# A hybrid decoder layer: second tile's projections by half rows, first experts from 64 sums, three last gathers split

## The reference

```python
def token_mix(x, positions, w_in, conv_w, conv_b, dt_bias, a_log, d_skip, norm_w, w_out):
    proj = x @ w_in
    q, k, v, iq, ik, iw, z, xbc, dt = jnp.split(proj, SPLIT_POINTS, axis=-1)
    attn = dsa_attention(q, k, v, iq, ik, iw, positions)
    ssd = ssd_mixer(z, xbc, dt, conv_w, conv_b, dt_bias, a_log, d_skip, norm_w)
    return jnp.concatenate([attn, ssd], axis=-1) @ w_out

def peer(h, wq, k1, k2, u, v):
    ...
    s1 = jnp.einsum('nhd,kd->nhk', q[:, :, 0], k1)
    s2 = jnp.einsum('nhd,kd->nhk', q[:, :, 1], k2)
    v1, i1 = lax.top_k(s1, 16)
    v2, i2 = lax.top_k(s2, 16)
    cand = (v1[..., :, None] + v2[..., None, :]).reshape(ntok, PEER_HEADS, -1)
    ...
    best, pos = lax.top_k(cand, 16)
    ...
    act = gelu(jnp.einsum('td,tkd->tk', xb, u[ib])) * gb
    return jnp.einsum('tk,tkd->td', act, v[ib])

x = layer_norm(ALPHA * x + token_mix(...))
x = layer_norm(ALPHA * x + peer(x, ...))
```

## Time and profile before

| | us |
|---|---|
| three runs | 791.58, 791.97, 792.56 |
| median | 791.97 |
| the profiled execution, whole | 791.58 |
| its span in the trace | 789.8 |

### The profile page before, as it was taken

One profiled execution on the slowest core, in us unless ns is written; L12 is line 12 of the kernel. 1 busy time (PEld: TensorE's weight loads), 2 busy tenths in 40 slices (PEclk: granted clock), 3 DMA queues, 4 the chain that ended last, 5 costly groups with the idle time before them and its releaser, 6 DMA issues.

```text
span 789.8 us, 10145 instructions
## 1 busy us (share of the span) xinstructions
PE 558.5 (71%) x3336; PEld 463.3 (59%) x3336; DVE 544.4 (69%) x1392; ACT 456.9 (58%) x818; POOL 280.6 (36%) x270
## 2 busy tenths in 40 slices
PE   8999999998977696758464546545454655465695
PEld 5486597767977596647353545545454645454642
DVE  1789479899745848484858586867667676767545
ACT  0244237878746676657565657656565656565633
POOL 0000004446633253434444444444434344434310
PEclk9999999999999899767877777677777677867699
DMA  8993019999999999999999999999999999999993
GB/s 318 387 394 159 27 55 336 397 418 421 421 418 420 421 420 420 422 422 420 422 419 424 418 422 421 421 421 421 422 420 423 420 424 420 423 420 423 421 420 126
DMA packets 49826, 301.09 MB, mean 381 GB/s; under 512 B 5221, under 2 KB 5877, under 8 KB 16249
## 3 DMA queue, kind: packets, MB, share of 16 engines
q0 software_dynamic: 37152, 268.45, 82.2%
q1 hardware_dynamic: 11448, 28.25, 9.5%
q10 hardware_dynamic: 1184, 3.88, 1.3%
HBM read 299.50 MB, written 1.06 MB: 381 GB/s over the span
## 4 chain that ended last, share of the span: by engine, by line
DMA 51%; DVE 18%; PE 16%; issue 7%; ACT 5%; POOL 2%; DVEq 0%; ACTq 0%; POOLq 0%
DMA arena<-in_expert_uv,expert 50%; PE bank L538 6%; DVE arena L1640 4%; PE bank L705 4%; PE bank L668 2%; POOL arena L498 2%; ACT arena L1089 1%; PE bank L649 1%; DVE big L1353 1%; PE bank L734 1%; ACT weight L1079 1%; ACT arena L999 1%; DMA arena<-in_w_idx 1%; PE bank L530 1%; DVE score L1623 1%
## 5 line engine op out<-in xcount | busy, mean ns | idle before, releaser
L705 PE MATMUL bank<-ident,arena 128*128 128x128 f32 x1920 | 306.0, 331 | 217.4 <-ACT arena L1089 217.4
L498 POOL DMA_INDIRECT arena<-in_expert_uv,expert x254 | 274.9, 1082 | 472.4 <-PE bank L705 244.7
L705 PEld LDWEIGHTS bank<-ident,arena 128*128 128x128 f32 x1920 | 284.2, 175 | 242.1 <-ACT arena L1089 239.8
L1640 DVE SCALAR_TENSOR_TENSOR arena<-x_sb,arena 128x1024 f32<-128x1024 f32 x256 | 307.3, 1224 | 171.2 <-DMA arena<-in_expert_uv,expert 170.9
L1089 ACT ACTIVATE arena<-arena,weight 128x1024 f32<-128x1024 f32 x240 | 257.0, 1138 | 2.2
L1074 ACT ACTIVATE gelu<-dots 128x4 f32<-128x4 f32 (+2 forms) x80 | 16.3, 204 | 222.8 <-DVE arena L1640 222.1
L1079 ACT ACTIVATE weight<-gelu,gate 128x1 f32<-128x1 f32 x256 | 56.4, 285 | 3.6
L538 PE MATMUL bank<-arena,x_t 128*128 128x512 f32 (+1 forms) x128 | 52.6, 563 | 1.3 <-DMA arena<-in_w_idx 1.3
L538 PEld LDWEIGHTS bank<-arena,x_t 128*128 128x128 f32 x128 | 24.3, 196 | 23.5 <-issue 20.1
L734 PE MATMUL bank<-arena,mid 128*128 128x512 f32 x64 | 28.6, 597 | 1.4 <-ACT mid L1086 1.4
L550 PE MATMUL bank<-x_t,arena 128*128 128x128 f32 x256 | 29.3, 276 | 0.0
(11 more groups left out here) (244 smaller groups left out, 518.7 us busy)
## 6 DMA issues: line engine op xcount, KB each, us to landing
arena<-in_w_in SPq DMA_DIRECT2D x5, 2048.0 KB, 20.4
arena<-in_w_out SPq DMA_DIRECT2D x2, 2048.0 KB, 19.9
arena<-in_expert_uv,expert POOLq DMA_INDIRECT x254, 26.7
wq_homes<-in_peer_wq SPq DMA_DIRECT2D x2, 1024.0 KB, 15.5
mix<-in_peer_wq SPq DMA_DIRECT2D x2, 1024.0 KB, 9.9
big<-in_peer_wq SPq DMA_DIRECT2D x2, 1024.0 KB, 8.9
x_sb<-in_w_q ACTq DMA_DIRECT2D x1, 1024.0 KB, 10.1
ln_gb<-in_w_q ACTq DMA_DIRECT2D x1, 1024.0 KB, 12.6
```

Of the source, the lines that this page charges most:

```text
L498: pool.indirect_dma_start(out=arena[:, slot * SLOT:(slot + 1) * SLOT], out_offset=None, in_=expert_uv, in_offset=bass.IndirectOffsetOnAxis ...
L705: last = mm(banks[2 * tile + k // 4][:, (k % 4) * P:(k % 4 + 1) * P], lhsT=arena[:, at + k * P:at + (k + 1) * P], rhs=ident[:, :], is_tran ...
L1640: ins = stt(rows, x_rows[:, bass.ds(tile * D_MODEL, D_MODEL)], 1.0, rows, ALU.mult, ALU.mult, accum_out=dots[:, parity, j:j + 1])
```

## The change

- `project_xbc` for tile 1 becomes `project_xbc_rows`: contraction step outside, column block inside, so that after half the steps the even slot is free. A semaphore `half_weights_read` counts this for xbc0, xbc1, z and v; slots 10, 12, 14 and 4 wait for it and no longer for the whole job.
- Three steps of xbc0 stand where one column block stood, a fourth where `carry_state` stood. `T_b` and `carry_state`, with their copies on ACT, come later. The second half of v, `carry_state` and the transposes of the probabilities change places with sums of slots.
- `first_slots`: slot 4 is the seventh, slot 1 the tenth.
- `name_first_pairs`: the first eight experts are named from the 8 x 8 sums of the best 8 of each side, before the next 8 are searched. (The best 8 of all 256 sums are among these 64.)
- Both convolutions of tile 1 stand behind the first dots.
- The last three gathers are split into u and v halves, not two.

```diff
-    start = [10, 11, 12, 13, 14, 15, 1, 10, 11, 12, 13, 5, 4, 14, 15, 0]
...
+    start = [10, 11, 12, 13, 14, 15, 4, 10, 11, 1, 12, 13, 5, 14, 15, 0]
...
+        HALVES_READ = {10: 1, 12: 2, 14: 3, 4: 4}
...
+                        elif slot in HALVES_READ:
+
+                            pool.wait_ge(half_weights_read, HALVES_READ[slot])
...
-            gather_unit(UNITS - 1, 1, SLOTS - 2)
+            gather_unit(UNITS - 1, 1, SLOTS - LAST_APART)
...
+                    if job in (("proj_z", 1), ("proj_v", 1)) and k == KT // 2 - 1:
+                        last.then_inc(half_weights_read, 1)
...
+            def project_xbc_rows(t, n, ks=range(KT)):
+
+                job = ("proj_xbc", t, n)
+                if ks[0] == 0:
+                    wait_bank(pe, job)
+                for k in ks:
+                    for c in range(4):
+                        last = mm(bank(job)[:, c * P:(c + 1) * P], lhsT=weight_rows(f"xbc{n}", k)[:, c * P:(c + 1) * P],
+                                  rhs=x_t[:, k, t * P:(t + 1) * P], start=k == 0 and c == 0, stop=k == KT - 1, skip_group_check=True)
+                    if k == KT // 2 - 1:
+                        last.then_inc(half_weights_read, 1)
...
-                    carry_state()
+                    project_xbc_rows(1, 0, range(3, 4))
...
-            transposes(("T_b",), [xbc[:, 4 + g, 0:P] for g in range(GROUPS)])
+            project_xbc_rows(1, 0, range(0, 3))
             logits_of(1, range(0, 2))
-            project_xbc(1, 0, range(0, 1))
...
-            project_xbc(1, 0, range(1, 4))
-            project_xbc(1, 1)
+            project_xbc_rows(1, 0, range(4, KT))
+            project_xbc_rows(1, 1)
             project(("proj_z", 1), "z", 1)
             running_sums(1)
+            transposes(("T_b",), [xbc[:, 4 + g, 0:P] for g in range(GROUPS)])
+            project(("proj_v", 1), "v", 1, ks=range(0, 4))
...
+            def name_first_pairs():
+
+                few = view(mid, 2048, 8, 8)
+                link(tt(few, top_v[:, 0, 0:8].unsqueeze(2).broadcast_to([P, 8, 8]),
+                        top_v[:, 1, 0:8].unsqueeze(1).broadcast_to([P, 8, 8]), ALU.add))
...
+                name_experts(0, range(0, 8), 8).then_inc(first_experts, 1)
```

## The result

| | us, median | lowest to highest | runs |
|---|---|---|---|
| kernel before | 791.58 | 790.02 to 792.56 | 7 |
| changed kernel | 794.89 | 793.31 to 795.26 | 7 |

The ratio of the times is 1.0041 (95% interval 1.0030 to 1.0051): **3.3 us slower**, outside the forecast range and on the side that was given 14%. The profiled execution took 794.75 us, with a span of 793.0 us, against 789.8.

The account below looks back on a forecast made before the run. The DMA stream of 256 gathers of 1 MB at about 420 GB/s was taken as the bound. Span 789.8 - 0.3 (25th gather) + 0.2 (tail) = 789.7 us, median forecast 791.9 us, eight in ten 789.8 to 793.9.

Parts of the forecast that it names:

- the side that was given 14%: Whole kernel: the chance 0.14 that the change makes it slower by more than 0.2%, 1.6 us here.
- First gather: Chain up to the first gather's issue: 0.4 + 2.1 + 1.0 = 3.5 us earlier, at 114.1 us.
- Slots by halves: Gathers behind the first, released by half projections: third at 116.7 us, seventh at 130.7 us instead of 133.3.
- The stand-still: PE ahead of tile 1's attention: waits 2.72 us for ACT's copies from 146.15 us; attention then takes 3.6 us.
- Where the lead goes: 19th to 25th gathers, behind tile 1's attention: of 3.5 us of lead, 0.3 us is left at the 25th landing.
- the engines ran dry: DMA at the 21st gather: lag falling to 6.8 us with gaps would show the forecast wrong on the slower side.
- Third split: Tail, last three gathers split: PE starts its last run 0.2 us later, waiting for value halves.
- The sum: Whole kernel: span 789.8 - 0.3 + 0.2 = 789.7 us, forecast for the median 791.9 us.
- the wait for the probabilities grows: PE ahead of attention: attention ending at 154.2 us or later, by a second ACT stall, gives 793.6 to 795; 11%.
- An earlier chain: Order after the first sums earlier than worked out: attention starts by 151 us, time 790.0 us; chance 22%.
- The fixed cost of splits: Tail: each split gather pays a fixed cost, one half-landing of 1.24 us, time 793.1 us; chance 3%.

Follow-up runs that it names:

- fill12: Changed kernel with 12 spare products of the identity on PE between the transposes of the probabilities and attention: 789.97 us, ratio 0.9991 to the kernel before.
- swap: Changed kernel with the transposes of the probabilities ahead of the sum of slots 5 and 6: 789.05 us, ratio 0.9988 to the kernel before.
- name_first: Kernel before with only the first eight experts named from 64 sums, ahead of the second search: 789.68 us, ratio 0.9989.
- swap_state_apart2: Changed kernel with the state's products, then the sum of slots 5 and 6, behind the probabilities' transposes, and two split gathers: 787.60 us, ratio 0.9958 to before.
- apart3: Kernel before with the last three gathers split instead of two, nothing else: 791.23 us, ratio 1.0006.
- late_probs: Kernel before with only the transposes of the probabilities moved directly ahead of attention, ACT's copies behind that of v: 796.32 us, ratio 1.0068.
- state_only: Changed kernel with only the state's two matmuls moved between the transposes of the probabilities and attention: 791.36 us, ratio 1.0003 to the kernel before.
- apart2: Changed kernel with the last two gathers split instead of three: 793.21 us, ratio 1.0033 to the kernel before.

## Why the prediction was wrong

**First gather: right.** 114.1 us forecast, 113.65 found. The 64 wide operations, priced at 0.21 us between two neighbours, took 0.20 to 0.22 us. One reading was off: the row cited for a step of 0.2175 us gives 12.67/56 = 0.226 us, which over 12 steps is 0.1 us.

**Slots by halves: right.** The third to seventh gathers were forecast at 116.7, 120.1, 123.5, 127.0 and 130.7 us and came at 116.28, 119.80, 123.24, 126.67 and 130.50. DVE's expert numbers of the second unit came at 149.89 us (150.1).

**The stand-still: right in place and length, wrong in price.** I had PE stand still for 2.72 us ahead of the attention (2.88 found), starting at 146.15 us (145.84), and wrote next: "Attention takes 3.6 us more: 152.6 us". **This is the step that failed.** The 3.68 us of the earlier trace rows is a duration at a clock of 1.00, of an engine that had been working without a gap. I carried it over to the far side of a wait of 2.7 us. Between 100 and 220 us PE's longest waits were 1.14 and 1.15 us, and behind them the clock was 1.00. This is the first, behind line 1060 of ACT near 135 us:

```profile
134.00:136.00 2.00, 0.86 (x8) 0.62 (x7) 1.85 (x8) 1.76 (x4) 1.70 (x2) 1.00 1.01 418
136.00:140.00 4.00, 4.00 (x25) 2.91 (x24) 3.56 (x21) 3.72 (x8) 1.19 (x2) 1.00 1.00 346
```

The text gave 3.6 us for the attention as if this held for 2.7 us too, and no bound from above. That longer waits are not harmless stood in the trace of before. Its next long one, at 227 us, is 4.05 us, and the clock behind it is 0.50 for 3.4 us:

```profile
227.12 5.41 PE L705 MATMUL bank<-ident,arena 128*128 128x128 f32 x32 [4.05 <-ACT arena L1089]
...
228.00:231.00 3.00, 3.00 (x16) 2.84 (x15) 1.23 (x2) 2.83 (x5) 1.59 (x2) 0.50 1.01 414
```

The page of before has it too, in the clock by slice:

```profile
PEclk9999999999999899767877777677777677867699
```

In the long stream, where PE waits for ACT again and again, it is mostly 6 to 8 tenths. Waits up to 1.68 us kept the clock there and those from 3.47 us on lost it, so the trace of before left 2.7 us open, and the attention needed two prices. The second was there to be worked out: at half speed it is twice 3.68, 7.4 us, 3.7 us more, and it took 7.09. The Trainium skill names the effect: in TensorE: Matmul & The Clock Gate, Why this matters for your kernels, a long idle gap between bursts of matmuls is what throws the engine back to its lower clock. The trace agrees, with 0.50 behind 2.88 us. No rival of the prediction let the one long wait that the change adds touch the clock.

**Where the lead goes: right, with the wrong starting point.** Everything behind the attention shifted with its end, as written. The 19th, 21st, 23rd and 25th gathers came 4.0, 4.0, 4.0 and 4.0 us behind the forecast (167.73, 173.92, 179.70, 184.89), for an attention 3.2 us late (148.72 + 7.09 = 155.81 for 152.6) and matmuls behind it that ran slow until 158.6 us. The lag from issue to landing fell to 6.2 us for the 21st, 7.9 for the 25th: the engines ran dry, which the text named as the sign of a forecast wrong on the slower side. With the clock kept, in fill12, the 25th landed 0.4 us sooner than before (0.3 forecast).

**Third split: right in sign, mis-sized.** Forecast 0.2 us, measured 0.34 to 0.43. The halves landed where they should (the 254th's value half 5.0 us behind the 253rd gather, the last whole one); PE started 0.15 us after that landing, which my sum left out, and the half landed 0.05 us later than in it.

**The sum.** Span 793.0 against 789.8: the 253rd gather lands 2.8 us later (775.65 for 772.88), and from there to the end it is 17.35 us instead of 16.92. The 25th had been 3.5 us later, so 0.7 us came back within the stream; I did not follow where.

**The rival that happened** is "the wait for the probabilities grows", which gave 793.6 to 795 and decides from an attention that ends at 154.2 us. It ended at 155.8 and the time is 794.89. But I had it "need a second stall" of ACT, and gave it 11% for that. No second stall came: ACT's copies took 2.74 us, as in the earlier trace rows. The wait was only 0.16 us longer than worked out; what it does to the engine behind it made the microseconds. "An earlier chain" (22%) was refuted for this kernel, and is what swap, name_first and swap_state_apart2 are: an attention that ends before 151 us, and a gain of 0.9 to 3.3 us by the ratios (swap's interval reaches 1.0001). The fixed cost of splits fell with apart3.

## What to carry to other kernels

A wait that a change puts on TensorE costs its own length and, if it is long, the clock of what follows: take a duration behind a new wait at both clock levels, and let the trace's own waits say which applies (in the kernel before 1.68 us or less kept the fast one, 3.47 us or more did not). Before a producer and its consumer are put side by side, count what stood between them; here one sum of 1.75 us moved by one line turned 3.3 us of loss into a time no slower than before, and into 1.8 us of gain with two splits. And where buffers are used again, bytes started early count only as far as the step that frees the buffers comes early: follow that step, not the first transfer.

## What was not expected of the hardware

- PE's clock fell after stand-stills of 2.01, 2.50, 2.57 and 2.88 us in six profiled executions of six, and not after 1.13 us or less; further on in the traces it was still 1.00 behind a wait of 1.93 us.
- The fall comes late and not at a fixed distance: 0.3 us ahead of the attention's first matmul in the changed kernel, 1.3 us behind it in late_probs, 2.0 in state_only and 2.2 in apart2. So the same 32 matmuls took 7.09, 5.95, 5.51, 5.32, 5.31 and 5.07 us from one profiled execution to the next. The runs of state_only lie 4.3 us apart and those of fill12 1.4 us, but those of the kernel before, with no such stand-still, 3.2 us, so scatter alone is no sign of a lost clock.
- It stays down under full load, and not for a fixed time: in the changed kernel from 148.4 to 158.6 us, with PE busy from 148.72 us on, but for 3.4 us behind the 4.05 us wait of the kernel before.
- Dead matmuls in a wait can pay: 2.84 us of them gave back some 4 us.
